# Attention by pairs of heads, two accumulators for weight tiles in the mix, and rows of h 448 words long

## The chip, the cores and the metric

The kernel runs on one core of one Trainium2 chip. The metric is the time of one execution on the device in microseconds (us). The core has five engines with a queue each: TensorE (PE, with its weight loads PEld), VectorE (DVE), ScalarE (ACT), GpSimd (POOL) and SyncE (SP, which issues most transfers). Each runs its own queue in order and they meet through semaphores.

## The reference

One inference step of a two-layer hybrid trunk, width 1024, on 128 context tokens and 256 latent tokens (384 columns in all). Each layer is: feed-forward (1024 to 2816 to 1024, SwiGLU), token mixing, feed-forward, each with a modulated RMS norm before it. Mixing projects h to the inputs of four branches and four gates, runs the branches, and sums them under the gates:

```
proj = h @ w_in
a_o = neighbourhood / dense attention, 4 heads of 64
b_o = windowed attention with sink, 4 heads, 2 key heads
c_o = hyena (long convolution by transforms)
d_o = differential attention, 4 heads, two maps of 32 each
y   = sum over branches of sigmoid(gate_b) * (branch_b @ w_branch_b), then @ w_out
```

Context tokens read 128 context keys. Latent tokens read 384 keys: their own 256 and 128 cached ones. All is float32.

## The kernel before

Activations lie transposed: channels on the 128 partitions, the 384 tokens along the row. The program is a list of phases (`phases`): per layer `norm`, three times `up` and `down`, `norm`, `mix`, `norm`, three times `up` and `down`. Every weight is a tile of 128 x 1024 words (1280 for the fused gate and branch tiles). A tile is loaded by SP into one of four slots of `raw`, rounded to `hi` by ACT (L563), and `lo = raw - hi` is made by DVE (L826, for wide tiles partly by POOL). `tile` (L1431) then does three fp32r matmuls per block of 128 rows: hi by h_hi, hi by h_lo, lo by h_hi. h_hi and h_lo have rows of `H_PITCH` = 400 words per block; the inputs of `down` and of the output projection (g_hi, g_lo) have rows of 384 words. In the feed-forwards after the first, the matmuls read 386 columns (two more carry the shift). A tile accumulates in one of four PSUM banks (`bank[n % RING]`), and `ready` waits for the drain of tile n - 4.

`mix` follows one list of steps, `mix_plan`, that all engines walk through in the same order. It spreads the tiles, cut in four parts of six matmuls (`parts`), between the small steps; `paced` deals out the parts in proportion to the numbers that stand between small steps. The stages are: four projection tiles before the norm is known, the filters of hyena under ten projection tiles, neighbourhood attention (NA) under eight, windowed (SWA) and differential attention (DF) under the first 16 fused tiles, hyena under the next eight, eight more, and the eight tiles of `out`. Steps that copy or round a weight tile (`feed`) and that drain a gate (`gate`) are put in by `staged`.

Attention goes one head and one block of 128 queries at a time, 12 units `u` for a type, 36 a layer. A unit is these steps: `scores` (PE matmul of 64 rows by 128 columns into `ps_s`; two matmuls of 32 rows, in two steps, for DF; then on DVE bias or mask and the maximum L1208, on ACT the exponential L754), `probs` (DVE: reciprocal L1224 and scaling L1234, or L1230 and L1231 for DF), `turn` (PE transposes L1681 into `ps_t`, ACT copies to `prT` L762), `values` (PE L1698, 128 rows by 64 columns into a half of `ps_o`). `vk` turns v and k to tokens by rows in `ps_t`; `rope` (L1654, L1190 to L1192) rotates q and k with `ps_br`; `short` (L1256, L1260) is hyena's short convolution on DVE; `subnorm`, `subinv` (L1244) and `subout` normalize the output of DF. `subnorm` (L1706) is two matmuls of 64 rows by 64 columns, each on its own rows and its own columns of TensorE.

The constants `kk` hold the transforms of hyena (`K_CS`, `K_SS`, 1024 words) and are loaded once.

Of the kernel before, what the change touches and what calls it, by code (L numbers as in the profile page):

```python
# [33 lines left out]
P = 128  # L34
T = T_CTX + T_DEN
TB = T // P
# [12 lines left out]
H_PITCH = T + 16  # L49
# [24 lines left out]
K_CS = K_SP + P  # L74
K_SS = K_CS + 512
K_NTN = K_SS + 512
K_TM = K_NTN + 3
K_COLS = K_TM + 3

# [86 lines left out]

def parts(tiles):

    return [(*t, part) for t in tiles for part in range(PARTS)]
# [18 lines left out]
def attention_steps(kind):  # L188

    out = []
    if kind == DF:
        out += [("scores", kind, 0, 0), 1.3, ("scores", kind, 0, 1), ("probs", kind, 0), 1.5]
        for u in range(12):
            if u + 1 < 12:
                out.append(("scores", kind, u + 1, 0))
            if u < 6:
                out.append(("short", u))  # L200

            if 7 <= u < 7 + TB:
                out.append(("subinv", 0, u - 7))
            if u == 7 + TB:
                out.append(("subout", 0))
            out += [0.9, ("turn", kind, u), 0.9, ("values", kind, u), 0.1]
            if u + 1 < 12:
                out += [("scores", kind, u + 1, 1), ("probs", kind, u + 1)]
            out.append(1.5)
            if u % 6 == 5:  # L210
                out += [("square", u // 6), 0.6, ("subnorm", u // 6)]
        return out + [0.8] + [("subinv", 1, b) for b in range(TB)] + [0.6, ("subout", 1), 0.2]
    out += [("scores", kind, 0, 0), ("probs", kind, 0), 1.5]
    for u in range(12):
        if u + 1 < 12:
            out.append(("scores", kind, u + 1, 0))
        out += [1.0, ("turn", kind, u)]
        if u + 1 < 12:
            out.append(("probs", kind, u + 1))
        out += [1.2, ("values", kind, u), 0.2]  # L220
        if u % 6 == 5:
            out.append(("outs", kind, u // 6))
    return out


def staged(plan):
# [10 lines left out]
    for s in plan:  # L237
        tile = s[0] in ("proj", "fused", "out")
        if tile and s[-1] == PARTS - 1:
            flush(fed)  # L240
        out.append(s)
        if tile and s[-1] == 0:
            fed.append(("feed", *s))
            flush(gates)
        if s[0] == "turn" or s[0] in ("proj", "out") and s[-1] == 1:
            flush(fed)
        if s[0] == "fused" and s[-1] == PARTS - 1:
            gates.append(("gate", *s[1:]))
            if s[1:3] == (3, C - 1):
                flush(gates)  # L250
# [3 lines left out]
def mix_plan():  # L254
# [13 lines left out]
    cut = na.index(("values", NA, NA_EARLY))  # L268
    turns = [("vk", 2), ("vk", 3), ("vk", 4)] + [("rope", j) for j in range(7)]
    rest = []  # L270
    for s in na[cut:]:
        rest.append(s)
        if turns and isinstance(s, tuple) and s[0] == "values":
            rest += [0.5, turns.pop(0), 0.3]
# [4 lines left out]
    swa, df = attention_steps(SWA), attention_steps(DF)  # L279
# [3 lines left out]
    plan += paced(gate_parts[:until], swa + df)  # L283
# [18 lines left out]
def build(nc, w_main, w_fused, w_ada, c_rep, consts, vecs, lam, x_in, rope, bias, logdecay, kctx, vctx, mlp_w, mlp_w3, zt, dft,  # L302
          y_out, nk, nv):
    ctx = ExitStack()
    with ctx:
# [37 lines left out]
        th = q_na  # L343
        gated = v_all[:, 3:5, :]
# [36 lines left out]

        raw_row = pr[:, :, :].rearrange("p a t -> p (a t)")[:, 0:T + 2]
# [5 lines left out]
        bank = [ctx.enter_context(nc.psum_tensor(f"bank{i}", [P, 512], F32)) for i in range(RING)]  # L388
        ps_br, ps_s, ps_t, ps_o = (ctx.enter_context(nc.psum_tensor(n, [P, 512], F32)) for n in ("ps_br", "ps_s", "ps_t", "ps_o"))
# [13 lines left out]
        g_hi_ready, row_ready = sem("g_hi_ready"), sem("row_ready")  # L403
# [14 lines left out]
        rot_ready, rope_done = sem("rot_ready"), sem("rope_done")  # L418
        scores_ready, max_ready, exp_done, probs_ready = (
# [9 lines left out]
        t_index = {s: i for i, s in enumerate([s for s in plan if s[0] in ("vk", "turn", "subnorm", "ytok")])}  # L429
        T_PER = len(t_index)  # L430
        rounds = [s for s in plan if s[0] == "scores"]
        r_index = {s: i for i, s in enumerate(rounds)}
        R_PER = len(rounds)
        U_PER = 36
# [20 lines left out]
        def unit(u):  # L455
            return u // 6, (u // 3) % 2, u % 3
# [90 lines left out]
        def _(act):  # L547
# [86 lines left out]
            def up(p):  # L634
# [9 lines left out]
                for j in range(p.tiles):  # L644
# [3 lines left out]
                    if p.q == 0 and j % 2 == 0:  # L648
# [6 lines left out]
                        act.activation(sil[:, s, 0:T], bank[n % RING][:, 0:T], ACT.Silu).then_inc(silu_done, 1)  # L655
# [27 lines left out]
            def mix(p):  # L683
# [3 lines left out]
                for step in plan:  # L687
# [7 lines left out]
                    elif kind == "gate":  # L695
# [4 lines left out]
                        act.activation(th[:, n % 2, :], bank[at % RING][:, 0:T], ACT.Tanh, scale=0.5).then_inc(th_ready, 1)  # L700
# [26 lines left out]
                    elif kind == "vk":  # L727
                        j, t = step[1], T_PER * l + t_index[step]
                        act.wait_ge(t_ready, t + 1)
                        ps3 = ps_t[:, :].rearrange("p (k c) -> p k c", k=4)  # L730
                        act.activation(vt[:, 0:3, P * j:P * (j + 1)], ps3[:, 0:3, :], ACT.Copy).then_inc(act_order, 1)
                        order[0] += 1
                        act.activation(k_tok[:, j, :], ps3[:, 3, :], ACT.Copy).then_inc(t_free, 1)
                    elif kind == "scores":
                        _, ty, u, m = step
                        r = R_PER * l + r_index[step]
                        act.wait_ge(max_ready, r + 1)
                        b = unit(u)[2]
                        nk_ = keys(b)[1] - keys(b)[0]
                        nm = tiny[:, 8 + r % 4:9 + r % 4]  # L740
                        if ty == SWA:
                            head = unit(u)[0] + 2 * unit(u)[1]
                            order[0] += 1
                            act.activation(tiny[:, 20 + r % 4:21 + r % 4], vcol(V_SINK + 4 * l + head), ACT.Exp, bias=nm).then_inc(act_order, 1)
                        g = U_PER * l + 12 * ty + u
                        if ty == DF and m == 0:

                            act.wait_ge(probs_ready, g)
                        elif ty == DF:
                            act.wait_ge(t_ready, T_PER * l + turn_t(ty, u))  # L750
                        elif g > 1:
                            act.wait_ge(t_ready, T_PER * l + turn_t(ty, u - 1) if u else T_PER * l + turn_t(ty, 0))
                        dst = pr[:, m if ty == DF else u % 2, 0:nk_]
                        act.activation(dst, ps_s[:, 0:nk_], ACT.Exp, bias=nm, accum_out=tiny[:, 12 + r % 4:13 + r % 4]).then_inc(exp_done, 1)  # L754
                    elif kind == "turn":
                        _, ty, u = step
                        t, g = T_PER * l + t_index[step], U_PER * l + 12 * ty + u
                        act.wait_ge(t_ready, t + 1)
                        if g:
                            act.wait_ge(values_done, g)  # L760
                        nk_ = keys(unit(u)[2])[1] - keys(unit(u)[2])[0]
                        act.activation(prT[:, 0:nk_], ps_t[:, 0:nk_], ACT.Copy).then_inc(t_free, 1)  # L762
                    elif kind == "outs":
                        _, ty, blk = step
                        act.wait_ge(values_done, U_PER * l + 12 * ty + 6 * (blk + 1))
# [3 lines left out]
                    elif kind == "square":  # L769
                        act.wait_ge(values_done, U_PER * l + 12 * DF + 6 * (step[1] + 1))  # L770
# [23 lines left out]

            def turn_t(ty, u):

# [1167 lines left out]
```

## Time and profile before

| | us |
|---|---|
| median of 3 runs | 2117.59 (2116.0 to 2121.73) |
| the profiled execution | 2116.72 |
| its span, first to last instruction | 2114.9 |
| PE busy | 2019.4 (95%) |
| PEld busy | 1890.9 (89%) |
| DVE busy | 1460.5 (69%) |
| ACT busy | 795.1 (38%) |
| POOL busy | 451.8 (21%) |

So 1.8 us of the profiled execution lie outside the span. Matmuls overlap each other and the end of each is modelled, so the time that PE really gives to a step is read from one start to the next and not from durations. A float32 matmul shows as two records, a transpose or an fp32r matmul as one.

### The profile page before, as it was taken

Reading aid. Unit: us, or ns where it says so; the run is one execution under the profiler, and the core shown is the slowest. Engines: PE = TensorE matmul, PEld = TensorE weight load, DVE = VectorE, ACT = ScalarE, POOL = GpSimd, SP = SyncE. Lnnn points to the kernel's source line nnn. Section 1 sums busy time; section 2 is a strip of 40 time slices with the busy share of each in tenths; the row PEclk is TensorE's granted clock in tenths of the full one; section 3 lists DMA queues with packets and bytes.
Section 4 is the critical chain, followed back from the end, with each engine's and each line's share of the span. In section 5 each row is a group of like instructions: output and inputs, shape, how many; then the busy total and the mean of one; then the engine's idle time right before and its main releaser. Section 6 shows DMA issues by size and latency. Waiting matters only on the chain.

```text
span 2114.9 us, 29547 instructions
## 1 busy us (share of the span) xinstructions
PE 2019.4 (95%) x11000; PEld 1890.9 (89%) x11000; DVE 1460.5 (69%) x2438; ACT 795.1 (38%) x1313; POOL 451.8 (21%) x357
## 2 busy tenths in 40 slices
PE   6999998999899999999999999989899999999998
PEld 6999997877668999999999999978676799999998
DVE  7888888556575457888888788865657544684544
ACT  3323234333343344333353333633333423533333
POOL 2301013211124531010131111321122353210101
PEclk9999998999999999999999999999999999999999
DMA  7766664222112235666575666422211223544332
GB/s 306 261 227 226 223 200 137 81 84 74 63 63 77 99 130 193 203 205 203 175 242 193 204 198 200 141 97 86 78 63 63 67 83 105 183 157 137 120 130 80
DMA packets 82548, 309.60 MB, mean 146 GB/s; under 512 B 9428, under 2 KB 10890, under 8 KB 81536
## 3 DMA queue, kind: packets, MB, share of 16 engines
q1 hardware_dynamic: 80064, 299.29, 42.8%
q0 software_dynamic: 2368, 8.80, 1.3%
q8 instruction: 68, 1.11, 0.2%
q14 instruction: 48, 0.39, 0.1%
HBM read 305.18 MB, written 2.88 MB: 146 GB/s over the span
## 4 chain that ended last, share of the span: by engine, by line
PE 80%; DVE 12%; ACT 4%; issue 3%; DMA 1%; POOL 0%; SPq 0%; DVEq 0%; ACTq 0%; POOLq 0%
PE bank L1431 69%; PE ps_br L1431 2%; DVE lo L826 2%; PE ps_s L1672 2%; PE ps_o L1698 2%; ACT hi L563 1%; DVE tiny L1208 1%; ACT pr L754 1%; DVE areaG L1260 1%; DVE tiny L1223 1%; DVE areaO L946 1%; ACT prT L762 1%; PE ps_t L1681 1%; PE ps_t L1616 1%; DMA areaM<-w_ada 1%
## 5 line engine op out<-in xcount | busy, mean ns | idle before, releaser
L1431 PE MATMUL bank<-h_hi,hi 128*128 128x384 f32 (+1 forms) x2272 | 802.1, 353 | 16.0 <-POOL h_lo L1333 10.5
L1431 PE MATMUL bank<-h_lo,hi 128*128 128x384 f32 (+1 forms) x2272 | 773.1, 340 | 0.0
L1431 PE MATMUL bank<-h_hi,lo 128*128 128x384 f32 (+1 forms) x2272 | 772.7, 340 | 0.0
L563 ACT ACTIVATE hi<-raw 128x1024 fp32r<-128x1024 f32 (+1 forms) x396 | 432.0, 1092 | 597.3 <-PE bank L1431 594.2
L826 DVE TENSOR_TENSOR lo<-raw,hi 128x1024 fp32r<-128x1024 f32 (+1 forms) x396 | 502.4, 1269 | 132.5 <-ACT hi L563 131.8
L1431 PEld LDWEIGHTS bank<-h_hi,hi 128*128 128x128 f32 x2272 | 431.8, 190 | 68.5 <-issue 45.2
L1431 PEld LDWEIGHTS bank<-h_lo,hi 128*128 128x128 f32 x2272 | 431.8, 190 | 1.1
L1431 PEld LDWEIGHTS bank<-h_hi,lo 128*128 128x128 f32 x2272 | 432.6, 190 | 0.0
L1310 POOL TENSOR_TENSOR g_lo<-areaF,g_hi 128x384 f32 x88 | 108.2, 1230 | 873.0 <-ACT g_hi L642 873.0
L1431 PE MATMUL bank<-g_hi,hi 128*128 128x384 f32 x832 | 279.6, 336 | 5.4 <-DVE g_lo L981 4.4
L1431 PE MATMUL bank<-g_hi,lo 128*128 128x384 f32 x832 | 278.7, 335 | 0.0
L1431 PE MATMUL bank<-g_lo,hi 128*128 128x384 f32 x832 | 278.6, 335 | 0.0
L1341 POOL TENSOR_TENSOR lo<-raw,hi 128x640 fp32r<-128x640 f32 x64 | 124.3, 1942 | 254.9 <-ACT hi L563 254.9
L1034 DVE SCALAR_TENSOR_TENSOR areaM<-areaM,areaO 128x1024 f32<-128x1024 f32 x128 | 169.2, 1322 | 0.0
L1431 PEld LDWEIGHTS bank<-g_hi,hi 128*128 128x128 f32 x832 | 156.7, 188 | 7.5 <-issue 4.1
L1034 DVE SCALAR_TENSOR_TENSOR areaO<-areaM,areaO 128x1024 f32<-128x1024 f32 x128 | 159.0, 1242 | 0.0
L1431 PEld LDWEIGHTS bank<-g_lo,hi 128*128 128x128 f32 x832 | 156.8, 188 | 0.0
L1431 PEld LDWEIGHTS bank<-g_hi,lo 128*128 128x128 f32 x832 | 156.6, 188 | 0.0
L1043 DVE SCALAR_TENSOR_TENSOR x<-bank,coef,x 128x128 f32<-128x128 f32 x224 | 82.7, 410 | 85.3 <-PE bank L1431 85.3
L754 ACT ACTIVATE pr<-ps_s,tiny 128x384 f32<-128x384 f32 (+1 forms) x96 | 48.6, 506 | 160.4 <-DVE tiny L1208 160.0
L1319 POOL TENSOR_TENSOR areaF<-areaF 128x384 f32<-128x384 f32 x47 | 70.9, 1508 | 121.1 <-ACT areaF L577 120.4
L1002 DVE TENSOR_TENSOR areaF<-bank,prT 128x386 f32<-128x386 f32 x66 | 36.6, 555 | 64.8 <-PE bank L1431 64.8
(231 smaller groups left out, 1830.4 us busy)
## 6 DMA issues: line engine op xcount, KB each, us to landing
raw<-w_main SPq DMA_DIRECT2D x332, 512.0 KB, 4.0
areaM<-w_ada SPq DMA_DIRECT2D x134, 512.0 KB, 3.5
raw<-w_fused SPq DMA_DIRECT2D x64, 640.0 KB, 3.9
areaG<-w_ada SPq DMA_DIRECT2D x7, 512.0 KB, 12.6
areaO<-c_rep SPq DMA_DIRECT2D x3, 1024.0 KB, 5.5
areaE<-bias POOLq DMA_DIRECT2D x2, 1024.0 KB, 6.1
x<-x_in SPq DMA_DIRECT2D x1, 1536.0 KB, 9.4
areaE<-w_ada SPq DMA_DIRECT2D x3, 512.0 KB, 15.4
```

The source lines that it names most:

```text
L563: act.activation(hi[:, slot, 0:width(base)], raw[:, slot, 0:width(base)], ACT.Copy).then_inc(hi_ready, 1)
L754: act.activation(dst, ps_s[:, 0:nk_], ACT.Exp, bias=nm, accum_out=tiny[:, 12 + r % 4:13 + r % 4]).then_inc(exp_done, 1)
L826: dve.tensor_tensor(lo[:, slot, 0:w], raw[:, slot, 0:w], hi[:, slot, 0:w].bitcast(F32), ALU.subtract).then_inc(lo_ready, 1)
L1002: dve.tensor_tensor(gf[:, s, :], b[:, 0:T + 2], rstd_one, ALU.mult).then_inc(drained, 1)
L1034: last = dve.scalar_tensor_tensor(out, ada_raw[slot], 1.0, cond_rows[:, g, :], ALU.mult, ALU.mult, accum_out=mod[:, a, g:g + 1])
L1043: last = dve.scalar_tensor_tensor(xs, bank[n % RING][:, t0:t1], coef[:, 2, c, g:g + 1], xs, ALU.mult, ALU.add)
L1310: pool.tensor_tensor(g_lo[:, at, :].rearrange("p a t -> p (a t)"), gf[:, s, 0:T], g_hi[:, at, :].rearrange("p a t -> p (a t)").bitcast(F32 ...
L1319: pool.tensor_tensor(sq[:, 0, :], sq[:, 0, :], sq[:, c, :], ALU.add).then_inc(sq_sum, 1)
L1341: pool.tensor_tensor(lo[:, slot, POOL_FROM:1280], raw[:, slot, POOL_FROM:1280], hi[:, slot, POOL_FROM:1280].bitcast(F32), ALU.subtract).th ...
L1431: last = pe.matmul(dst, wt[:, slot, w], ac[:, c, 0:cols], start=c == 0 and k == 0, stop=c == chunks - 1 and k == 2)
L1672: pe.matmul(ps_s[:, 0:k1 - k0], q[a:e, blk, P * b:P * (b + 1)], kt[a:e, kb, k0:k1], start=True, stop=True).then_inc(scores_ready, 1)
L1698: last = pe.matmul(ps_o[64 * hh:64 * hh + 64, P * b:P * (b + 1)], vt[:, ch, col:col + 64], prT[:, P * i:P * (i + 1)], start=i == 0, stop=i ...
```

## The change

Attention goes by pairs of heads, 6 pairs `w` a type and 18 a layer. In `scores` the two heads' matmuls follow each other on different rows of TensorE and into different banks (four matmuls for DF, in one step); bias, mask and maximum are one DVE instruction for both; `turn` transposes both; in `values` the heads' matmuls alternate on different columns. `attention_steps` writes a new order: for NA and SWA the values of pair w - 2, the turn of pair w - 1 and the scores of pair w stand together; SWA and DF are one list. Scores and turns use four banks together (`ps_att`), so tiles of the mix from the fifth on have two accumulators, and `ready` waits for the last tile in the same bank. `vk` moves to `ps_br`. `H_PITCH` is 448. The two large transforms leave `kk`: POOL loads them (`late`, 512 KB) at the first gate of each layer.

```diff
-H_PITCH = T + 16
+H_PITCH = 448
+def bank_of(n):
+    for n0 in MIX_N0:
+        if n0 + RAW_TILES <= n < n0 + N_PROJ + 5 * C:
+            return n % 2
+    return n % RING
-def attention_steps(kind):
+def attention_steps(*kinds):
+    units = [(kind, w) for kind in kinds for w in range(6)]
+    out, waiting, turned = [], None, None
+    def values(unit):
+        out.append(("values", *unit))
+        if unit[1] % 3 == 2:
+            out.append(("square", unit[1] // 3) if unit[0] == DF else ("outs", unit[0], unit[1] // 3))
+    for kind, w in units:
+        if turned is not None:
+            values(turned)
+            turned = None
+        if waiting is not None:
+            out.append(("turn", *waiting))
+            turned, waiting = waiting, None
+            if kind == DF:
+                out.append(1.2)
+                values(turned)
+                turned = None
+        out.append(("scores", kind, w))
+        if kind == DF:
+            out += [1.0, ("short", w), 2.0]
+            if w == 4:
+                out += [("subinv", 0, b) for b in range(TB)]
+            if w == 5:
+                out.append(("subout", 0))
+            out += [("probs", kind, w), 1.8, ("turn", kind, w)]
+            if w == 3:
+                out.append(("subnorm", 0))
+            out.append(1.6)
+            turned = (kind, w)
+        else:
+            out += [2.4, ("probs", kind, w), 1.6]
+            waiting = (kind, w)
...
-        if s[0] == "turn" or s[0] in ("proj", "out") and s[-1] == 1:
+        if s[0] == "probs" or s[0] in ("proj", "out") and s[-1] == 1:
             flush(fed)
...
-    cut = na.index(("values", NA, NA_EARLY))
+    cut = na.index(("scores", NA, NA_EARLY))
...
-    plan += paced(gate_parts[:until], swa + df)
+    plan += paced(gate_parts[:until], both)
...
+        prT_2 = {NA: areaO[:, 768:768 + T], SWA: areaE[:, 768:768 + T], DF: areaE[:, 768:768 + T]}
+        pr_2 = areaE[:, 0:768].rearrange("p (a t) -> p a t", t=T)
+        ps_att = ctx.enter_context(nc.psum_tensor("ps_att", [P, 4, 512], F32))
+        banks = [bank0, bank1, ps_att[:, 0, :], ps_att[:, 1, :]]
+        ps_s, ps_t = ps_att[:, 2, :], ps_att[:, 3, :]
...
+                            red = dve.tensor_reduce(nm, ps_att[:, at:at + 2, 0:k1 - k0], AX_X, ALU.max, negate=True)
...
+                        for hh in range(2):
+                            dst = pr[:, hh, 0:nk_]
+                            last = dve.tensor_scalar(dst, dst, rr[:, hh:hh + 1], None, ALU.mult)
+                            if ty == DF:
+                                link(last)
+                                last = dve.scalar_tensor_tensor(dst, pr_2[:, hh, 0:nk_], rr[:, 2 + hh:3 + hh], dst, ALU.mult, ALU.add)
...
+                    elif step[:2] == ("gate", 0) and step[2] == 0:
+                        pool.wait_ge(kv_out, 16 * 6 * (l + 1))
+                        pool.dma_start(late, consts[:, K_LATE:K_ALL]).then_inc(late_in, 16)
...
-                if base >= RING:
-                    pe.wait_ge(drained, base - RING + 1 + 4 * rep)
+                if LAST_IN_BANK[base] >= 0:
+                    pe.wait_ge(drained, LAST_IN_BANK[base] + 1 + 4 * rep)
...
+                        for m in range(2 if ty == DF else 1):
+                            for hh in range(2):
+                                a = 64 * hh + 32 * m
+                                e = a + (32 if ty == DF else 64)
+                                last = pe.matmul(ps_att[:, att_set(ty, w) + 2 * m + hh, 0:k1 - k0], q[a:e, blk, P * b:P * (b + 1)], kt[a:e, kb, k0:k1],
+                                                 start=True, stop=True)
...
                         for i, ch in enumerate(chunks):
-                            last = pe.matmul(ps_o[64 * hh:64 * hh + 64, P * b:P * (b + 1)], vt[:, ch, col:col + 64], prT[:, P * i:P * (i + 1)],
-                                             start=i == 0, stop=i == len(chunks) - 1)
+                            for hh, src in enumerate((prT, prT_2[ty])):
+                                col = (64 * (2 * blk + hh), 256 + 64 * hh, 384 + 64 * (2 * blk + hh))[ty]
+                                last = pe.matmul(ps_o[64 * hh:64 * hh + 64, P * b:P * (b + 1)], vt[:, ch, col:col + 64], src[:, P * i:P * (i + 1)],
+                                                 start=i == 0, stop=i == len(chunks) - 1)
```

## Rows read from the trace of the kernel before

**Rows 1.** The page, busy time, share of the span and instructions of each engine.

```profile
PE 2019.4 (95%) x11000; PEld 1890.9 (89%) x11000; DVE 1460.5 (69%) x2438; ACT 795.1 (38%) x1313; POOL 451.8 (21%) x357
```

**Rows 2.** Stretches of attention: window, length, busy PE PEld DVE ACT POOL, clock, DMA.

```profile
427.00:656.00 229.00, 208.85 (x1070) 160.55 (x1069) 137.14 (x308) 88.28 (x208) 48.82 (x32) 0.99 0.22 71
1451.00:1682.00 231.00, 211.41 (x1068) 162.61 (x1067) 136.93 (x306) 88.28 (x208) 48.83 (x32) 0.98 0.22 70
```

**Rows 3.** Waits of PE, 427 to 656 us: total, times, longest.

```profile
PE ps_o L1698 <- ACT prT L762: 11.1, 17, 1.3
PE ps_s L1672 <- ACT pr L754: 3.3, 6, 1.8
```

**Rows 4.** Groups of PE by shape, 427 to 656 us: records, busy us, mean ns, idle before.

```profile
L1698 PE MATMUL ps_o<-prT,vt 128*64 128x128 f32 x168 | 26.7, 289 | 11.3 <-ACT prT L762 11.1
L1672 PE MATMUL ps_s<-kt,areaG 32*128 32x384 f32 x32 | 14.7, 540 | 2.6 <-ACT pr L754 2.6
L1672 PE MATMUL ps_s<-kt,areaG 64*128 64x384 f32 x16 | 7.3, 535 | 0.0
L1672 PE MATMUL ps_s<-kt,q_swa 64*128 64x384 f32 x16 | 7.2, 533 | 0.1
L1672 PE MATMUL ps_s<-kt,areaG 32*128 32x128 f32 x16 | 3.8, 315 | 0.7 <-ACT pr L754 0.7
```

**Rows 5.** PE in order of time: start, length; values, scores, then a tile.

```profile
438.61 0.87 PE L1698 MATMUL ps_o<-prT,vt 128*64 128x128 f32 x6
439.41 0.49 PE L1672 MATMUL ps_s<-kt,areaG 64*128 64x128 f32 x2
439.83 0.44 PE L1431 MATMUL bank<-h_hi,hi 128*128 128x384 f32 x1
440.11 0.34 PE L1431 MATMUL bank<-h_lo,hi 128*128 128x384 f32 x1
```

**Rows 6.** PE in order of time: a subnorm, scores of DF, a tile.

```profile
611.25 0.86 PE L1706 MATMUL ps_t<-areaE,kk 64*64 64x384 f32 x4 [0.25 <-ACT areaE L774]
612.04 0.91 PE L1672 MATMUL ps_s<-kt,areaG 32*128 32x384 f32 x2
612.88 0.44 PE L1431 MATMUL bank<-h_hi,hi 128*128 128x384 f32 x1
```

**Rows 7.** PE in order of time: the first matmul of five feed-forward phases.

```profile
150.80 0.33 PE L1431 MATMUL bank<-h_hi,hi 128*128 128x384 f32 x1
...
218.40 0.33 PE L1431 MATMUL bank<-g_hi,hi 128*128 128x384 f32 x1
...
251.71 0.33 PE L1431 MATMUL bank<-h_hi,hi 128*128 128x384 f32 x1
...
897.95 0.34 PE L1431 MATMUL bank<-h_hi,hi 128*128 128x386 f32 x1
...
965.98 0.34 PE L1431 MATMUL bank<-g_hi,hi 128*128 128x384 f32 x1
```

**Rows 8.** Groups of DVE and ACT by shape, 427 to 656 us.

```profile
L1208 DVE TENSOR_REDUCE tiny<-ps_s 128x1 f32<-128x384 f32 x32 | 17.8, 555 | 6.9 <-PE ps_s L1672 6.4
L1260 DVE SCALAR_TENSOR_TENSOR areaG<-areaG,vv 128x255 f32<-128x255 f32 x12 | 7.1, 593 | 0.4
L1231 DVE SCALAR_TENSOR_TENSOR pr<-pr,tiny 128x384 f32<-128x384 f32 x8 | 4.9, 618 | 0.3
L1244 DVE RECIPROCAL areaE<-areaE 128x128 f32<-128x128 f32 x4 | 3.8, 945 | 4.1 <-ACT areaE L778 4.1
L754 ACT ACTIVATE pr<-ps_s,tiny 128x384 f32<-128x384 f32 x32 | 18.5, 577 | 60.0 <-DVE tiny L1208 60.0
```

**Rows 9.** In order of time: the drain of the mix's sixth tile, its eighth's start.

```profile
374.16 0.55 DVE L1110 TENSOR_SCALAR areaG<-bank 128x384 f32<-128x384 f32 x1
...
376.40 0.33 PE L1431 MATMUL bank<-h_hi,hi 128*128 128x384 f32 x1
```

**Rows 10.** A stretch with a low clock, columns as in Rows 2.

```profile
1625.00:1640.00 15.00, 15.00 (x62) 11.78 (x62) 8.96 (x21) 7.12 (x14) 2.54 (x2) 0.76 0.15 44
```

More of the change, by code:

```diff
@@ L185, in paced @@
     return out + tiles[done:]
-def attention_steps(kind):
[L193 to L204, printed above, removed]
-                out.append(("subout", 0))
[L206 to L222, printed above, removed]
@@ new lines, in attention_steps @@
+def attention_steps(*kinds):
[22 more added lines that the diff above has]
+            if w == 5:
+                out.append(("subout", 0))
+            out += [("probs", kind, w), 1.8, ("turn", kind, w)]
[6 more added lines that the diff above has]
+            waiting = (kind, w)
+    if turned is not None:
+        values(turned)
+    if waiting is not None:
+        out.append(("turn", *waiting))
+        out.append(2.0)
+        values(waiting)
+    if DF in kinds:
+        out += [0.8, ("subnorm", 1), 1.0] + [("subinv", 1, b) for b in range(TB)] + [0.8, ("subout", 1), 0.4]
@@ L271, in mix_plan @@
     for s in na[cut:]:
-        rest.append(s)
-        if turns and isinstance(s, tuple) and s[0] == "values":
-            rest += [0.5, turns.pop(0), 0.3]
+        if isinstance(s, tuple):
+            rest.append(s)
+            if turns and s[0] == "scores":
+                rest.append(turns.pop(0))
+        elif turns:
+            rest += [s / 2, turns.pop(0), s / 2]
+        else:
+            rest.append(s)
     for s in turns:
@@ L343, in build @@
         th = q_na
+        late = areaG[:, 11 * T:11 * T + 1024]
         gated = v_all[:, 3:5, :]
@@ L427, in build, with pair_no, round_no, heads @@
         plan = mix_plan()
-        t_index = {s: i for i, s in enumerate([s for s in plan if s[0] in ("vk", "turn", "subnorm", "ytok")])}
+        t_index = {s: i for i, s in enumerate([s for s in plan if s[0] in ("turn", "subnorm", "ytok")])}
         T_PER = len(t_index)
[L431 to L434, printed above, removed]
+        U_PER, R_PER = 18, 24
+        def pair_no(l, ty, w):
+            return U_PER * l + 6 * ty + w
+        def round_no(l, ty, w, m=0):
+            return R_PER * l + 6 * ty + w + (w + m if ty == DF else 0)
+        def heads(ty, w, m=0):
+            return 2 * m if ty == DF else 2 * (w % 2)
+        def turns_before(step):
+            done = [t_index[s] + 1 for s in plan[:plan.index(step)] if s in t_index]
+            if step[1] != DF and step[2]:
+                done = done[:-1]
+            return max(done, default=0)
         FUSED0 = N_PROJ
@@ L739, in mix @@
+                        blk, b = unit(w)
                         nk_ = keys(b)[1] - keys(b)[0]
[L740 to L745, printed above, removed]
@@ L1214, in mix @@
-                        red.then_inc(max_ready, 1)
-                    elif kind == "probs":
-                        _, ty, u = step
-                        nk_ = keys(unit(u)[2])[1] - keys(unit(u)[2])[0]
-                        r = R_PER * l + r_index[("scores", ty, u, 1 if ty == DF else 0)]
-                        dve.wait_ge(exp_done, r + 1)
-                        rs = tiny[:, 12 + r % 4:13 + r % 4]
-                        rr = tiny[:, 16 + r % 4:17 + r % 4]
-                        if ty == SWA:
-                            link(dve.tensor_tensor(rs, rs, tiny[:, 20 + r % 4:21 + r % 4], ALU.add))
+                        dve.wait_ge(scores_ready, pair_no(l, ty, w) + 1)
@@ L1235, in mix @@
+                        last.then_inc(probs_ready, 1)
                     elif kind == "outs":
@@ new lines, in mix @@
+                        last.then_inc(scores_ready, 1)
+                    elif kind == "turn":
+                        _, ty, w = step
+                        b = unit(w)[1]
+                        pe.wait_ge(probs_ready, pair_no(l, ty, w) + 1)
+                        for hh in range(2):
+                            for i in range((keys(b)[1] - keys(b)[0]) // P):
+                                last = pe.transpose(ps_att[:, att_set(ty, w) + hh, P * i:P * (i + 1)], pr[:, hh, P * i:P * (i + 1)], ident)
```

201 lines of the change are left out of this document (97 added, 104 removed).

## The prediction

> **What bounds the kernel now.** I read the page first. PE is busy 95% of the span and DVE 69% [rows 1], so a microsecond counts if it is taken from PE's stream of matmuls, or from PE's waiting. The table by stretches then shows where PE's time is not weight tiles: attention lasts 229 us in the first layer and 231 in the second, with PE busy for 209 and DVE for 137 [rows 2]. In the waits of that stretch PE waits most for ACT's copy of the turned probabilities, 11.1 us, and for the exponentials, 3.3 [rows 3]. The groups by shape give the counts, and the timeline the true cost of a step, from its start to the next start, since matmuls overlap. A stretch of attention divides as follows. Eight projection tiles and 16 fused ones are 8 x 24 + 16 x 30 = 672 fp32r matmuls, at 0.175 us 118 us. The attention matmuls are below. The rest, some 35 us, is breaks in the stream and waits.
>
> **Scores.** A single head's matmul of 384 keys costs 612.88 - 612.04 = 0.84 us, one of 128 keys 439.83 - 439.41 = 0.42 [rows 5, 6]. The 64 records with 384 keys are 32 matmuls [rows 4]; 16 more have 128 keys (those of 32 rows are 8 of them). Before: 32 x 0.84 + 16 x 0.42 = 33.6 us a layer. After, 12 heads of NA and of SWA and four maps of each DF pair lie on rows of their own. Does TensorE run such matmuls at once? This trace has one case, subnorm: two matmuls of 384 columns on separate rows and columns take 612.04 - 611.25 = 0.79 us together [rows 6], less than one head's scores. I take that: a step costs what one matmul costs, so 8 + 4 large steps and 4 + 2 small ones, 12 x 0.84 + 6 x 0.42 = 12.6. Gain 21.0. Bounds: 0 if separate rows alone don't overlap, 21.0 if fully.
>
> **Values.** Three matmuls take 439.41 - 438.61 = 0.80 us [rows 5], 0.133 a record, so 168 records [rows 4] are 22.4 us. Heads alternate on separate columns; at the same overlap 11.2 goes. Bounds 0 and 11.2, by the same row.
>
> The Trainium skill speaks against full overlap. The trace's pair takes 0.79 us where two singles would be 1.68 [rows 6]. "TensorE: Matmul & The Clock Gate", section "Measured speedup vs the span model", has measured 3.07 times for four row tiles and 2.38 for three column tiles, under 0.8 of ideal. By 0.8, an estimate from that page, a pair gains 1.6 times, and the forecast would be some 13 us later.
>
> **Turns** keep their transposes: 0.
>
> **Breaks.** After a small step the first tile matmul takes 440.11 - 439.83 = 0.28 us to the next instead of 0.175 [rows 5], and a step of fewer rows or columns costs about as much on entering. Before, a layer's attention has 120 such steps (48 scores, 36 turns, 36 values), partly adjacent, in about 90 breaks with vk and rope. After, NA and SWA have one break a pair, DF two, and vk, rope and subnorm some 12: 36. That is 54 x 0.1 = 5.4, and 18 to 20 fewer entries, 1.8: together 7. Bounds 4 and 9.
>
> **Waits.** PE's idle time in the stretch is 229.0 - 208.9 = 20 us [rows 2]. The new order gives each pair a longer cover, but its chain is longer too. For a large SWA pair: mask and maximum over two heads at most 3 x 0.56, two exponentials 1.2, two scalings at most 0.62 each, and about 0.8 for short instructions and hand-overs (an estimate): 4.9 us. Its cover: the 4.0 in the list are 3.9 parts (65 parts on a sum of 66.6), at 6 x 0.175 us each 4.1, one branch part 1.05 and the values before the turn, 5.9 together. No wait, save where a gate (tanh and drain, two instructions of the size of those above, 1.1) falls between. For a large DF pair: two maxima over two heads 2.0, then on DVE `short` 2.7 (five linked instructions of at most 0.6, the longer shift takes 0.59), then four scalings of at most 0.62, 2.5 together, 7.2 [rows 8], against a cover of 6.2 (4.7 parts and the branch part's share). So 1 us for each of four pairs, about 3.5 more in the one that has three reciprocals of 0.945 ahead [rows 8], and 1 for gates that land badly: 8 to 9. In NA vk and ropes stand two or three to a pair with 1.6 parts, 1.7 us, between, while DVE or ACT still works on the scores: about 5 in all. With 1 for the end, 15 us of waits. That replaces the 20: gain 5, bounds -6 and +14.
>
> **Two accumulators.** A tile now waits for the drain two tiles back. The nearest case in both mixes is the eighth tile: it starts at 376.40 and the sixth is drained at 374.71, 1.7 us before [rows 9]. Fused tiles already wait for the gate before them ahead of their branch part. So 0. If cover goes, a late drain costs its lateness once; I allow 3 us for both layers.
>
> **The load of `late`.** On POOL at the first gate: one more issue and a wait for stores issued some ten tiles before. Behind it in POOL's queue stands its half of the next wide tile, wanted two tiles and more later; POOL is busy for 49 of the 229 us [rows 2]. The data are wanted after 16 fused tiles. 0, and a few us if the stores land late.
>
> **Rows of 448 words.** A phase on h in the first feed-forward has 384 matmuls in 218.40 - 150.80 us, 176.0 ns each; the one on g has 192 in 33.31, 173.5. With 386 columns it is 384 in 68.03, 177.2 [rows 7]. The instructions are alike and the weights come from the same tiles; the rows of h start every 1600 bytes, no multiple of 256, those of g every 1536, which is one, and 1792 is one too. I take that as the cause. First feed-forward: 1056 x 2.5 ns = 2.7 us. The other three: 3168 x 2.8 = 8.9, of which I take half, since no row of g has 386 columns. Mix: 2592 x 2.5 = 6.5. Sum 13.7; bounds 0 and 19. PE has no gap in these phases, so it all counts.
>
> The Trainium skill would make it nothing: "SBUF — State Buffer", section "Door 1: The DMA port swizzle", has lines of 16 bytes, and 1600 is a multiple of 16 as well. The trace disagrees as far as h and g differ, 2.5 ns [rows 7]; by the page alone the time would be 14 us later.
>
> **The sum.** A layer: 21.0 + 11.2 + 7 + 5 = 44; two layers 88; with 13.7, 102. The profiled execution took 2116.7 (span 2114.9 and 1.8 around it): 2014.7. It lies 0.9 below the median of 2117.6, so 2015 to 2016; I say 2015.
>
> **Rivals.**
> - A. The pairs overlap only in part or not at all. For it: the one pair in the trace differs in rows and columns both, scores only in rows, values only in columns. With values serial 2015 + 22 = 2037; with both serial 2015 + 64 = 2079. Chance 0.14, mostly near 2037.
> - B. The wait replaces the work: two heads' chain isn't covered, PE waits at every turn. For it: DF's chain exceeds its cover already. Against: SWA's is covered. At 1.2 us more for each of 36 pairs: 2058. Chance 0.15.
> - C. The rows of 448 words do nothing: 2029. Chance 0.10.
> - D. Slower. PE's waits now come in one piece ahead of a turn, and the clock falls to its lower level of 1.2 GHz. In one stretch of 15 us, after waits of this kind, the granted clock was 0.76 on average [rows 10], so 7.2 us at half, 3.6 lost. For each of 36 pairs that is 130: 2145. It decides from 28 falls on. Against: the clock is 0.98 or more over both stretches, with 20 us of waits in each [rows 2]. Chance 0.05.
>
> **How the numbers follow.** The forecast has 0.56. The low end is the sum with waits of 5 a layer and all of the 448 words: 2015 - 20 - 5 = 1990, and 1988 with the breaks' bound. The high end takes in C, A with serial values and B up to its price: 2060. Left out are both pairs serial, D, and cases that add up. The cases of A, B and C are all faster than before; 0.3% (6 us) is what a measurement of this kernel can tell from no change. Forecast and C give 0.66 of faster; of A and B 0.02 may end within it, the rest is faster, and D is slower: faster 0.93, same 0.02, slower 0.05.
>
> **What would show it.** Records of two heads' scores starting within some 10 ns of each other, and a pair step of about 0.85 us before the next start; twelve records of values in 0.8; attention stretches of 182 to 188 us; PE's waits found before turns, on DVE, and no longer before values, on ACT; h phases at 173.5 to 174.5 ns a matmul; no wait of a tile on a drain. The forecast is wrong if a pair's scores take 1.6 us, if PE's idle time in a stretch is over 30 us, or if h phases keep their 176.

## The result and the profile after

The kernel after takes 2076.27 us (median of 4 runs, 2075.5 to 2080.09) against 2116.8 before: a ratio of 0.9812, interval 0.980 to 0.9824, 40 us less. Forecast were 102 less, and the time lies 16 us above the range's high end. The profiled execution took 2080.09, the longest of the four (span 2078.3). The difference is clear of noise.

The same stretches of attention, columns as in [rows 2]:

```profile
426.00:641.00 215.00, 179.07 (x1060) 153.43 (x1059) 126.34 (x232) 84.56 (x202) 43.52 (x33) 0.91 0.24 76
1437.00:1648.00 211.00, 174.97 (x1057) 150.12 (x1056) 126.08 (x232) 84.47 (x202) 43.44 (x33) 0.94 0.24 77
```

The edges of these windows lie a few us off the same place in each kernel. In the traces, from the first matmul behind the filters to the end of the 16th fused tile, the same work lasts 228 and 231 us before, 217 and 213 after.

PE's work did shrink, from 208.9 and 211.4 us to 179.1 and 175.0. But the part in which PE is idle grew from 20 us to 36, where 15 were forecast, and the granted clock fell from 0.99 and 0.98 to 0.91 and 0.94. Waits of PE in the first stretch, the three largest, answering to [rows 3]:

```profile
PE ps_att L1732 <- DVE pr L1277: 19.7, 5, 7.9
PE ps_att L1732 <- DVE pr L1274: 7.1, 7, 2.5
PE ps_br L1479 <- DVE areaM L1167: 4.4, 1, 4.4
```

L1732 is the turn, L1277 the last scaling of a DF pair, L1274 that of NA and SWA. So the waits are where the forecast put them, before turns and on DVE, but in DF they are far longer; the third is a branch part that waits for a gate queued behind such a chain. Added up wait by wait along the first stretch, NA has 5.3 us (forecast were about 5), SWA 4.1 (forecast was none but for gates), and DF 26.5 (forecast were 8 to 9). The second stretch has the same waits within 0.2 us a line.

The steps themselves, PE in order of time: scores of a large NA pair and the step behind; scores of a large DF pair and the tile behind; then, at 449, the first two of the 12 records of one large values step and the turn behind. (A large pair has 384 keys, a small one 128.)

```profile
440.44 0.92 PE L1723 MATMUL ps_att<-kt,areaG 64*128 64x384 f32 x4
441.29 0.55 PE L1690 MATMUL ps_br<-kk,areaG 128*128 128x128 f32 x3
...
544.88 0.93 PE L1723 MATMUL ps_att<-kt,areaG 32*128 32x384 f32 x8
545.74 0.44 PE L1479 MATMUL bank<-h_hi,hi 128*128 128x384 f32 x1
...
449.17 0.32 PE L1750 MATMUL ps_o<-prT,vt 128*64 128x128 f32 x1
449.18 0.32 PE L1750 MATMUL ps_o<-areaO,vt 128*64 128x128 f32 x1
...
449.98 0.88 PE L1732 MATMUL ps_att<-kk,pr 128*128 128x128 f32 x6
```

Two scores matmuls take 441.29 - 440.44 = 0.85 us together and four take 545.74 - 544.88 = 0.86, where one took 0.84 [rows 6]; two heads' values take 449.98 - 449.17 = 0.81, where one head's took 0.80 [rows 5].

Now the DF pair with the longest wait. Its scores are issued at 597.72; DVE in order of time after them, then ACT, POOL and PE:

```profile
598.72 1.82 DVE L1253 TENSOR_REDUCE tiny<-ps_att 128x2 f32<-128x768 f32 x2 [1.82 <-PE ps_att L1723]
600.45 0.47 DVE L1300 TENSOR_SCALAR areaG<-areaG,vv 128x384 f32<-128x384 f32 x1
600.96 1.77 DVE L1304 SCALAR_TENSOR_TENSOR areaG<-areaG,vv 128x127 f32<-128x127 f32 x4
603.34 2.21 DVE L869 TENSOR_TENSOR lo<-raw,hi 128x640 fp32r<-128x640 f32 x1 [0.60 <-ACT hi L617]
605.47 0.54 DVE L1167 SCALAR_TENSOR_TENSOR areaG<-areaG,ps_br 128x384 f32<-128x384 f32 x1
605.93 2.91 DVE L1288 RECIPROCAL areaE<-areaE 128x128 f32<-128x128 f32 x3
608.88 0.62 DVE L1290 SCALAR_TENSOR_TENSOR areaE<-areaE,tiny 128x384 f32<-128x384 f32 x1
...
611.32 0.62 DVE L1277 SCALAR_TENSOR_TENSOR pr<-areaE,tiny,pr 128x384 f32<-128x384 f32 x1
...
601.95 1.28 ACT L617 ACTIVATE hi<-raw 128x1280 fp32r<-128x1280 f32 x1
...
603.31 1.55 POOL L1385 TENSOR_TENSOR lo<-raw,hi 128x640 fp32r<-128x640 f32 x1 [5.34 <-ACT hi L617]
...
612.00 1.33 PE L1732 MATMUL ps_att<-kk,pr 128*128 128x128 f32 x5 [7.92 <-DVE pr L1277]
```

From 598.72 to the end of the last scaling at 611.9 the chain takes 13.2 us, and PE's cover had run out 7.92 us before the turn. The forecast had about 10 for this pair (7.2 and three reciprocals) against a cover of 6.2; the cover was five parts, 5.3 us. Besides what the forecast counted there stands a weight tile's split, L869. It first waits for ACT's rounding of that tile, which ACT starts at 601.95, behind the four exponentials; then it takes 2.21 us, since POOL splits its half beside it. The pair's exponentials had ended at 602.1. L1167, the drain of a gate, is in the chain too.

The clock follows such waits. Four windows in a row, columns as in [rows 2]:

```profile
596.00:602.00 6.00, 6.00 (x39) 5.04 (x37) 3.73 (x7) 2.60 (x10) 1.00 (x1) 0.95 0.00 0
602.00:608.00 6.00, 2.07 (x12) 1.75 (x11) 5.29 (x7) 2.77 (x4) 3.46 (x3) 0.90 0.23 73
608.00:614.00 6.00, 2.00 (x9) 2.00 (x10) 4.50 (x9) 0.42 (x2) 0.56 (x1) 0.50 0.17 52
614.00:620.00 6.00, 6.00 (x38) 5.03 (x36) 0.00 (x0) 0.45 (x2) 0.00 (x0) 0.75 0.26 97
```

PE is busy for 2 of the 6 us to 608. The clock falls to its lower level of 1.2 GHz shortly before 608 (0.90 in that window), stays there to 614 (0.50) and returns to 2.4 GHz in the window behind the turn (0.75).

The rows of h, the first matmul of phases as in [rows 7]:

```profile
150.60 0.33 PE L1479 MATMUL bank<-h_hi,hi 128*128 128x384 f32 x1
...
217.16 0.33 PE L1479 MATMUL bank<-g_hi,hi 128*128 128x384 f32 x1
...
882.80 0.34 PE L1479 MATMUL ps_att<-h_hi,hi 128*128 128x386 f32 x1
...
950.63 0.34 PE L1479 MATMUL ps_att<-g_hi,hi 128*128 128x384 f32 x1
```

384 matmuls take 66.56 us, 173.3 ns each (before 176.0), and with 386 columns 67.83, 176.6 (before 177.2).

### The profile page after: what moved, and what is told of

Same layout as the page of the kernel before. It is cut to its first block, busy times and chain, and to the rows that moved or that the text cites. A ratio compares the mean times of both kernels' runs of the same rounds, so it can differ in the third digit from the quotient of the medians.

```text
span 2078.3 us, 29068 instructions
## 1 busy us (share of the span) xinstructions
PE 1949.2 (94%) x11000; PEld 1868.2 (90%) x11000; DVE 1442.3 (69%) x2290; ACT 787.5 (38%) x1301; POOL 446.3 (21%) x359
## 4 chain that ended last, share of the span: by engine, by line
PE 80%; DVE 13%; ACT 4%; issue 2%; DMA 0%; SPq 0%; POOL 0%; DVEq 0%; ACTq 0%; POOLq 0%
PE bank L1479 44%; PE ps_att L1479 26%; PE ps_br L1479 2%; DVE pr L1274 1%; DVE lo L869 1%; PE ps_att L1732 1%; ACT hi L617 1%; PE ps_att L1723 1%; ACT pr L800 1%; DVE tiny L1253 1%; PE ps_o L1750 1%; DVE areaG L1304 1%; DVE pr L1277 1%; DVE areaO L989 1%; DVE areaE L1288 1%
## 5 line engine op out<-in xcount | busy, mean ns | idle before, releaser
L869 DVE TENSOR_TENSOR lo<-raw,hi 128x1024 fp32r<-128x1024 f32 (+1 forms) x396 | 501.5, 1267 | 121.0 <-ACT hi L617 120.2
L1479 PE MATMUL bank<-h_hi,hi 128*128 128x384 f32 (+1 forms) x1536 | 543.9, 354 | 18.9 <-POOL h_lo L1377 8.7
L1479 PE MATMUL bank<-h_lo,hi 128*128 128x384 f32 (+1 forms) x1536 | 524.6, 342 | 0.0
L1479 PE MATMUL bank<-h_hi,lo 128*128 128x384 f32 (+1 forms) x1536 | 524.0, 341 | 0.0
L1479 PEld LDWEIGHTS bank<-h_hi,lo 128*128 128x128 f32 x1536 | 295.0, 192 | 0.0
L1479 PE MATMUL ps_att<-h_hi,hi 128*128 128x386 f32 (+1 forms) x736 | 248.7, 338 | 2.5 <-DVE lo L869 2.5
L1479 PE MATMUL ps_att<-h_hi,lo 128*128 128x386 f32 (+1 forms) x736 | 248.5, 338 | 0.0
L1479 PE MATMUL ps_att<-h_lo,hi 128*128 128x386 f32 (+1 forms) x736 | 248.5, 338 | 0.0
L1479 PEld LDWEIGHTS ps_att<-h_hi,hi 128*128 128x128 f32 x736 | 138.7, 188 | 2.8 <-DVE lo L869 2.8
L1479 PEld LDWEIGHTS ps_att<-h_hi,lo 128*128 128x128 f32 x736 | 138.6, 188 | 0.0
L1479 PEld LDWEIGHTS ps_att<-h_lo,hi 128*128 128x128 f32 x736 | 138.6, 188 | 0.0
```

The costliest lines, as they stand in the source:

```text
L869: dve.tensor_tensor(lo[:, slot, 0:w], raw[:, slot, 0:w], hi[:, slot, 0:w].bitcast(F32), ALU.subtract).then_inc(lo_ready, 1)
L1479: last = pe.matmul(dst, wt[:, slot, w], ac[:, c, 0:cols], start=c == 0 and k == 0, stop=c == chunks - 1 and k == 2)
```

## The experiments

Each ratio is to the kernel before, timed beside the run. Differences are those of the ratios, times 2117 us; each is good to some 4 us. The kernel after stands at 0.9812.

| run | ratio (interval) | us | against |
|---|---|---|---|
| e1 rows of 400 words | 0.9861 (0.9844 to 0.9877) | +10 | after |
| e2 rows of 416 words | 0.9841 (0.9825 to 0.9857) | +6 | after |
| e3 splits held back | 0.9693 (0.9676 to 0.9709) | -25 | after |
| e4 also `short`, reciprocals moved | 0.9607 (0.9591 to 0.9623) | -43 | after |
| e5 scores on the same rows | 0.9973 (0.9964 to 0.9983) | +34 | after |
| e6 heads' values in turn | 0.9864 (0.9846 to 0.9883) | +11 | after |
| e7 e4, GpSimd waits at every pair | 0.9569 (0.9553 to 0.9585) | -8 | e4 |
| e8 e4 with e5 and e6 | 0.9791 (0.9773 to 0.981) | +39 | e4 |
| e9 only GpSimd's half waits | 0.9704 (0.9686 to 0.9722) | -23 | after |
| e10 two parts more of cover | 0.9803 (0.9785 to 0.982) | -2 | after |
| e11 e7, reciprocals later still | 0.9578 (0.956 to 0.9595) | +2 | e7 |
| e12 e11, 0.6 parts more of cover | 0.9584 (0.9566 to 0.9602) | +1 | e11 |

**Rows of h (e1, e2).** `H_PITCH = 448` becomes 400 and 416.

> The kernel after with rows of h 400 words long again, all else kept. Theory (rows of h that start on a multiple of 256 bytes are read faster): phases with 384 columns return from 173.33 to 176.1 ns a matmul, those with 386 from 176.64 to 177.2, fused tiles from 173.3 to 175.4 or so; 1056 x 2.7 + 3168 x 0.55 + 2592 x 2.1 ns = 2.9 + 1.7 + 5.4 = 10 us more than the kernel after, near 2086. Rival (the phases are faster because of where other buffers came to lie, or of the two accumulators): they stay at 173.3, no difference.

> Rows of h 416 words long, 1664 bytes: every second row starts on a multiple of 256 bytes, the others 128 bytes off. Theory (each row start off the multiple costs, on it nothing): with 1600 bytes one row of four lay on it and the mean was 2.73 ns more, so 3.64 for a row off it; with half of the rows on it 173.33 + 1.82 = 175.2 ns for 384 columns; 5 to 7 us more than the kernel after. Rival (a multiple of 128 bytes is enough): 173.3 ns, no difference. Rival (any row off 256 spoils its neighbours as well): 176, as at 400 words, 10 us.

First an h and a g phase of e1, then of e2:

```profile
151.69 0.33 PE L1479 MATMUL bank<-h_hi,hi 128*128 128x384 f32 x1
...
219.30 0.33 PE L1479 MATMUL bank<-g_hi,hi 128*128 128x384 f32 x1
```

```profile
151.78 0.33 PE L1479 MATMUL bank<-h_hi,hi 128*128 128x384 f32 x1
...
219.19 0.34 PE L1479 MATMUL bank<-g_hi,hi 128*128 128x384 f32 x1
```

67.61 us at 400 words, 176.1 ns a matmul, as before, though the other buffers of the two kernels differ; 67.41 at 416, 175.5 ns. The row length is the cause, and it is worth 10 us. My finer rule is not: with half of the rows on a multiple of 256 bytes instead of a quarter, 175.2 ns were due. With 386 columns 416 words read as fast as 448 (176.65 and 176.64 ns). What in the address counts stays open.

**What makes the turns late (e3, e4).** In `staged`, splits are held back while a pair is open; e4 moves two more steps.

```diff
+        if s[0] in ("scores", "probs"):
+            held = s[0] == "scores"
-        if tile and s[-1] == PARTS - 1:
+        if tile and s[-1] == PARTS - 1 and not held:
             flush(fed)
```

```diff
-            out += [1.0, ("short", w), 2.0]
+            out += [3.0]
+            out += [("probs", kind, w), ("short", w), 1.8, ("turn", kind, w)]
+            if w == 3:
+                out.append(("subnorm", 0))
             if w == 4:
                 out += [("subinv", 0, b) for b in range(TB)]
             if w == 5:
                 out.append(("subout", 0))
-            out += [("probs", kind, w), 1.8, ("turn", kind, w)]
-            if w == 3:
-                out.append(("subnorm", 0))
```

> The kernel after, with the splits of weight tiles held back between a pair's scores and its probabilities. Theory (in DF pairs the chain is late by what DVE does for a weight tile in it: 0.8 to 1.7 us of split and the wait for ACT's rounding, about 2 us, in some 5 pairs a layer): PE's idle time in an attention stretch falls from 36 us to 22 to 28, the fall of the granted clock in it gets shorter, and the time falls by 25 to 40 us, to 2036 to 2051. Rival 1 (the chain is too long by itself): idle stays over 32, the time falls by less than 8. Rival 2 (a split that is held back makes a later tile late): waits of tiles on the split appear, and the time is the same or longer.

> The edit of e3, and DF's `short` placed behind the probabilities' step, and the reciprocals of subnorm behind the turn. Theory (linked work on DVE ahead of the probabilities is what makes a turn late): PE's idle time in a stretch falls to 15 to 20 us, the granted clock stays up, and the time falls by 45 to 60 us, to 2016 to 2031. Rival 1 (the clock falls because of the pair steps themselves, not of waits): idle falls as said but the clock still shows some 30 us at half in each stretch; 2040 to 2055. Rival 2 (what is moved only comes late somewhere else): waits of `values` or of the branch part take the turns' place, less than 15 us gained.

The theory came out at its low end or just short of it: e3 gains 25 us where it had 25 to 40, with 27 us of idle time in a stretch; e4 gains 43 where it had 45 to 60 (2034.28 us, above its 2031). Which of e4's two moves, `short` or the reciprocals, gives the 18 us more was not tried apart. The stretches of e4:

```profile
424.00:619.00 195.00, 173.91 (x1083) 150.24 (x1082) 131.07 (x236) 86.25 (x203) 43.73 (x33) 0.97 0.26 86
1410.00:1606.00 196.00, 174.95 (x1088) 151.21 (x1088) 132.01 (x236) 86.27 (x203) 44.22 (x33) 0.97 0.26 86
```

Idle time is 21 us in each; between the same two places as above both stretches last 193 us. The clock is back at 0.97 with the pair steps unchanged: it had fallen because of the waits in the main. DVE is busier than in the kernel after, 131 us for 126, and the kernel is faster all the same; what counts is what stands ahead of the probabilities.

**Is the overlap worth less than it seemed (e5, e6, e8)?** `a = 64 * hh + 32 * m` becomes `a = 0` (e5), the two loops of the values change places (e6), and e8 is both on e4. In e5 and e8 every scores matmul of a step thus reads the rows of the first head (in DF those of its first map), and the second head's own scores are left out; number and shape of the matmuls stay.

> The kernel after with every scores matmul on the rows from 0 up (so that the values come from the wrong head; the work is the same in number and shape): two or four matmuls of a step can't run at once. Theory (the overlap is worth what the forecast took, 21.0 us a layer, and the waits of the turns come behind it and don't absorb it): a pair step takes 1.68 us instead of 0.85, a large DF step 3.4 instead of 0.86, and the time is 38 to 46 us over the kernel after, 2115 to 2122. Rival (PE would have waited for the chain anyway, so that the overlap's gain is partly lost in the waits): under 25 us more, near 2095.

> The kernel after with the values matmuls of one head all ahead of those of the other, so that only one of a step's places in the array works at a time. Theory: a large values step takes 1.5 to 1.6 us instead of 0.81, 11.2 us a layer, and since values stand behind the waits and in the cover of the next turn, part of it is hidden in the next wait: 10 to 20 us over the kernel after. Rival (two heads' matmuls overlap in this order too, because the second head's start before the first's end): under 5 us.

> The kernel of e4 with both overlaps undone: all scores on the rows from 0 up (values from the wrong head) and the values of one head ahead of the other's. Theory: 64 us a layer pair of lost overlap in all (21.0 + 11.2 a layer) less what the longer steps lie in waits: 50 to 64 us over e4, 2084 to 2098. Rival (overlap is worth less than the sum of its steps since turns are late anyway): 25 to 45, 2060 to 2079.

A large NA pair, then a large DF pair of e5:

```profile
441.06 1.55 PE L1723 MATMUL ps_att<-kt,areaG 64*128 64x384 f32 x4
442.55 0.55 PE L1690 MATMUL ps_br<-kk,areaG 128*128 128x128 f32 x3
...
552.15 2.84 PE L1723 MATMUL ps_att<-kt,areaG 32*128 32x384 f32 x8
554.92 0.44 PE L1479 MATMUL bank<-h_hi,hi 128*128 128x384 f32 x1
```

1.49 and 2.77 us instead of 0.85 and 0.86: on the same rows a matmul behind another costs 0.64, and only the last of a step the 0.84 of [rows 6]. I had expected 1.68 and 3.4. With 0.64 us for each of 8 pairs, 1.91 for each of 4 quads (the four matmuls of a large DF pair) and less for the small ones some 15 us a layer are at stake, 30 in all; 34 were measured. This is below the 38 to 46 of the theory, because the steps are shorter than it had them. But waits do absorb a part: PE's idle time falls from 36 and 36 us to 31 and 34. PE works 63 us of the two stretches at the lower clock instead of 46, 8 us lost, and that makes up for it. The values of one head ahead of the other's, e6, a part of one large step and the turn behind:

```profile
449.63 0.54 PE L1750 MATMUL ps_o<-prT,vt 128*64 128x128 f32 x3
449.91 0.32 PE L1750 MATMUL ps_o<-areaO,vt 128*64 128x128 f32 x1
450.01 0.27 PE L1750 MATMUL ps_o<-prT,vt 128*64 128x128 f32 x1
...
450.71 0.88 PE L1732 MATMUL ps_att<-kk,pr 128*128 128x128 f32 x6
```

1.08 us, not 1.5: the second head's records begin while the first's still run, so e6 takes the overlap away only in part. On e4 both together cost 39, where the theory had 50 to 64 and its rival 25 to 45. The number is the rival's, its reason is not: PE's idle time falls from 21 to 19 us in each stretch, so waits absorb 4 us in all; the steps by themselves cost 35 and not 64, and more time at the lower clock adds 8. The overlap is real in each version, and rival A is refuted.

**Contention (e9, e7).** In e9 GpSimd's half of a wide tile's split waits for an open pair's probabilities. In e7, on e4, GpSimd waits at the `probs` step of every pair. The edit of e9:

```diff
                     elif step[0] == "feed":
+                        if open_pair:
+                            pool.wait_ge(probs_ready, pair_no(l, open_pair[1], open_pair[2]) + 1)
                         split(p.n0 + tile_of(step[1:]) + AHEAD)
```

> The kernel after; only GpSimd's half of a wide tile's split waits, where it stands between a pair's scores and probabilities, for these probabilities. Theory (contention by itself lengthens the chain): in the first stretch of the kernel after, 14 VectorE instructions of the chain and of `short` had a GpSimd one beside them and took some 14 us more than their like; with most of that gone PE idles 5 to 8 us less a layer, and the time falls by 12 to 22 us, to 2054 to 2064. Rival (what is late is VectorE's own half of the split and its wait for ACT, contention hits only work that is hidden): less than 6 us.

> The kernel of e4, and GpSimd's half of a wide tile's split now waits until a pair's probabilities are scaled. Theory (a VectorE instruction that reads SBUF alone or twice doesn't go on until a GpSimd instruction beside it has ended: scalings of 0.42 and 0.62 us took 1.5 to 1.8 beside one): the scalings in the pair with three reciprocals take 2.1 us together instead of 4.5, the turn behind waits 2 us less, PE's idle time in a stretch falls from 21 to 16 to 18, and the time by 6 to 12 us, to 2022 to 2028. Rival (GpSimd's half only comes late for the tile that needs it, or collides with VectorE's own half of the split all the same): within 4 us of e4.

The first instruction of `short` in the kernel after, then in e9, groups of the first stretch; and e9's stretch:

```profile
L1300 DVE TENSOR_SCALAR areaG<-areaG,vv 128x384 f32<-128x384 f32 x6 | 5.3, 888 | 0.0
```

```profile
L1300 DVE TENSOR_SCALAR areaG<-areaG,vv 128x384 f32<-128x384 f32 x6 | 2.8, 472 | 0.0
...
425.00:627.00 202.00, 175.23 (x1063) 150.47 (x1062) 115.17 (x232) 84.34 (x201) 42.74 (x32) 0.94 0.25 81
```

DVE's busy time falls from 126 to 115 us with the same 232 instructions, idle time of PE from 36 to 27, and 23 us are gained by delaying another engine's work. That is nearly all that e3 gains. But e3 moves both halves of the split, GpSimd's too, so its 25 us do not show what DVE's own half and the wait for ACT cost by themselves; no run here moves these alone. Contention is the part that is shown. e7 is the best version here, 2024.29 us, 4.3% below before:

```profile
424.00:609.00 185.00, 168.49 (x1057) 146.44 (x1056) 121.11 (x230) 84.08 (x201) 49.36 (x32) 0.97 0.27 88
1404.00:1592.00 188.00, 171.45 (x1074) 149.25 (x1073) 122.71 (x233) 84.21 (x201) 49.37 (x32) 0.97 0.27 89
```

Stretches of 185 and 188 us (187 both, between the same two places) with 16 us of idle time are about what the forecast gave to the kernel after. Of SWA's 4.1 us of waits 1.2 are left.

**A longer cover instead (e10, e12).** `2.0` ahead of `probs` becomes `4.0`; in e12, on e11 (next section), `3.0` becomes `3.6`, and the `1.2` between a turn and its values becomes `0.6`.

> The kernel after with two parts more between a DF pair's scores and its probabilities, all else in its old order, splits included. Theory (a longer cover brings in more splits and gates too, so it gives less than its length, and the parts are missing from the covers of SWA): PE's idle time in a stretch falls from 36 to 25 to 30, and the time by 10 to 20 us. Rival (the chain is only too long, 2 parts of 1.05 us each for six pairs take 2.1 us from every late turn): idle falls to 20 to 24, the time by 25 to 35 us.

> The kernel of e11 with 0.6 parts more between each DF pair's scores and probabilities. Theory (some 2 us of waits before turns are left in DF, which 0.6 us of cover take by a third each): 1 to 4 us less than e11. Rival (what is left of PE's idle time is hand-overs and the branch part's wait for a gate): no difference.

The first stretch of e10 and PE's largest wait in it:

```profile
423.00:634.00 211.00, 175.88 (x1059) 151.91 (x1058) 123.89 (x231) 84.06 (x201) 44.33 (x32) 0.93 0.24 77
...
PE ps_att L1732 <- DVE pr L1277: 22.2, 6, 6.9
```

Two more parts a pair, and the wait is 22.2 us instead of 19.7, idle time 35. Both numbers I had written down were too good. In the pair with the longest wait, w = 4, the chain takes 13.2 us as before, but the cover is only one part, 1.0 us, longer, and the wait 1.0 shorter. w = 3 and w = 5 gain 0.7 us each, and w = 2 loses it all: it waits 5.3 us, for a branch part and its turn, instead of 2.9. That a part of a tile brings its share of splits and gates into such a chain is a likely reason, not a shown one. In e12 nothing is gained either (+1 us), as its rival had it.

**Reciprocals (e11).** `subinv` of the first block moves from behind the turn of w = 4 to behind the probabilities of w = 5.

> The kernel of e7 with the first three reciprocals of subnorm behind the probabilities of the last DF pair. Theory: in e7 they kept VectorE busy until 592.5 while that pair's scores stood ready, and its branch part and turn were late by 4 us; now these 4 us a layer go: 4 to 8 us less than e7, 2016 to 2020. Rival (the last gates wait for the branch's output, which comes later now): within 3 us of e7, or longer.

A miss, the rival's case. Of the branch part's wait at w = 5, 4.1 us in e7, 0.6 is left. But `square` of the second block has to wait for the branch's output of the first, which comes later, and the subnorm behind it waits 6.7 us in each layer:

```profile
PE ps_att L1764 <- ACT areaE L825: 6.7, 1, 6.7
```

## Why the prediction was wrong

Right were: scores and values (0.85, 0.86 and 0.81 us a step), no wait of a tile on a drain, the place of the waits, NA's waits, and the step from 176 to 173.3 ns. PE's busy time was nearly right: with the time lost to the lower clock taken out it falls from 206 to 167 us a layer, 39 less, where the forecast has 41.

The rule weighed against the overlap in the forecast (the Trainium skill, "TensorE: Matmul & The Clock Gate", section "Measured speedup vs the span model") gives 3.07 times for four row tiles. What this case's trace makes of it depends on what one compares with. Four matmuls took 0.86 us where one alone takes 0.84, 3.9 times as fast as four alone, and the kernel before had them alone, so the forecast's price was right. Against the same four behind each other on the same rows, 2.77 us in e5, it is 3.2 times, near the page's figure.

The step that failed is **Waits**: "For a large DF pair: [...] 7.2 together, against a cover of 6.2. So 1 us for each of four pairs", 15 us a layer in all. It was 36, of which DF has 26.5 and not 8 to 9. The list of the chain was incomplete. I put down what belongs to the pair and to `short`, as if DVE's queue held nothing else, and priced each instruction as if GpSimd stood still. Left out were the split of a weight tile, which `staged` flushes at a tile's last part even between scores and probabilities; DVE's wait for ACT's rounding, itself behind four exponentials; and the price of DVE's instructions beside GpSimd's. The means that I took hide it (L1260 has 593 ns in [rows 8], and 484 alone in e4; a scaling of "at most 0.62" takes 1.7 beside GpSimd). The runs take these away: of 36 us idle in a stretch e3 and e9 leave 27 each, e4 21 and e7 16. Rival B's 43 us are nearly the 42 by which the waits exceed the forecast, but it has them in each of 36 pairs: here three quarters are in DF's 12.

The second term is the **clock**. The forecast carried none of it, and rival D had it as all or nothing at 0.05. The two stretches were at the lower level for 37 and 27 us, before for 3 and 10. PE worked in 27.6 and 18.8 of these, before in 3.4 and 10.2: half of the difference, 16 us, is lost. A chain that is late for a few pairs is enough; it didn't take all 36. In e4, with 21 us of waits, 10 us a stretch are left.

The third is that of the **rows of 448 words**, 10 us instead of 13.7: with 386 columns the gain was 0.5 ns, not half of 2.8.

Together: 2 x 21 us of idle time, 16 of clock, 5 of PE's own work and 4 of the rows are 67, and the profiled execution lies 65 above the forecast. So these terms account for the miss within 2 us.

## What to carry to other kernels

When a chain is set against its cover, list what the engine's queue really holds between its first and last instruction, from the plan and from a like stretch of the trace: feeding work of other tiles, its waits for a third engine, and gates count in full. Take the duration of a DVE instruction that may run beside GpSimd's from its fastest and slowest records, not from the group's mean. Here more cover didn't help (2 us), while moving off-path work behind the chain gave 43 us and holding back GpSimd's share of it alone 23.

## What the runs showed of the hardware

DVE and GpSimd hold each other up. e4 in order of time, first DVE, then POOL:

```profile
586.98 0.99 DVE L1274 TENSOR_SCALAR tiny<-tiny 128x2 f32<-128x2 f32 x1
588.01 1.65 DVE L1277 TENSOR_SCALAR pr<-pr,tiny 128x384 f32<-128x384 f32 x1
589.70 1.77 DVE L1280 SCALAR_TENSOR_TENSOR pr<-areaE,tiny,pr 128x384 f32<-128x384 f32 x1
591.39 0.41 DVE L1277 TENSOR_SCALAR pr<-pr,tiny 128x384 f32<-128x384 f32 x1
...
586.94 1.01 POOL L1450 TENSOR_TENSOR areaM<-areaM,areaG 128x384 f32<-128x384 f32 x1 [3.64 <-DVE areaG L1170]
587.91 3.14 POOL L1388 TENSOR_TENSOR lo<-raw,hi 128x640 fp32r<-128x640 f32 x2
```

A scaling of two elements, 0.23 us alone, takes 0.99 and ends with GpSimd's instruction; the same L1277 takes 1.65 beside one and 0.41 behind. In the first stretch of e4, 16 scalings of 384 columns that began with GpSimd idle took 0.41 to 0.42 us, the eight others 1.65 to 1.78. It goes the other way too: GpSimd's half of a split takes some 1.55 us, and 2.2 where it began while DVE was at its own half. Maxima over PSUM (L1256, 0.95 us) show no difference, two of them beside GpSimd. The Trainium skill, "SBUF — State Buffer", section "Who interferes with whom", has this as an exclusive lock on a port pair that the two share, for instructions with two inputs in SBUF and for forms such as `tensor_scalar`; the trace agrees, 0.41 and 1.65 us for the same instruction.

Each of the five falls of the granted clock in the first stretch of the kernel after began inside a wait of PE: of 4.4, 2.9, 2.3, 7.9 and 4.6 us. Waits are not all of it: e8 has 19 us of idle time in each stretch and e4 21, but e8 was at the lower level for 17 us in each and e4 for 10, and one of e8's falls, at 566.0 us, has no wait of PE in the 6 us before it. What e8 has more of is matmuls on few rows or columns, one behind another; which of them counts wasn't tried.
